# Expert gates built by indirect accumulating transfers into tables in device memory, with all down rounds ahead of all up rounds

## What is computed

```python
q = (xt @ w_query).reshape(T, 8, 2, 128)                      # T = 256 tokens
scores = einsum('thpc,hpnc->thpn', q, sub_keys)               # 128 keys per half
vals, idx = lax.top_k(scores, 16)
cand = vals[..., 0, :, None] + vals[..., 1, None, :]          # 256 sums per head
top_vals, top_c = lax.top_k(cand.reshape(T, 8, 256), 16)
experts = i1 * 128 + i2                                       # 128 of 16384 per token
gates = softmax(top_vals)
y = sum_e gates[e] * gelu(expert_down[e] . x) * expert_up[e]
```

## Time and profile before

| | |
|---|---|
| median of 3 runs | 3400.38 us |
| the profiled execution | 3400.34 us |
| its span | 3398.5 us |
| PE busy | 3264.6 us (96%) |
| DVE, ACT, POOL busy | 59%, 44%, 11% |
| DMA | 594.66 MB, mean 175 GB/s |

### The profile page before, as it was taken

How to read it: one execution, slowest core, us unless ns; L and a number is a source line. 1 busy time by engine, 2 the same in 40 slices (tenths; PEclk the granted TensorE clock), 3 DMA queues, 4 the chain that set the end, 5 groups by cost and what they waited for, 6 DMA issues and landing times.

```text
span 3398.5 us, 43470 instructions
## 1 busy us (share of the span) xinstructions
PE 3264.6 (96%) x16266; PEld 2680.6 (79%) x16266; DVE 2016.6 (59%) x2347; ACT 1478.9 (44%) x1868; POOL 378.7 (11%) x261
## 2 busy tenths in 40 slices
PE   8999999988889999999889999999989999999998
PEld 7988787766667878888767888899877888888886
DVE  5444453898886454555887555655566554444444
ACT  5444344433334343433334434454545544434343
POOL 3100000000881000000783000000000000000000
PEclk9999899999999999999999999999999999999999
DMA  6644355555446666666445766665434555565554
GB/s 210 181 138 127 106 167 167 171 182 182 140 149 205 194 204 190 224 204 192 144 146 191 217 201 199 197 205 160 125 120 138 190 185 181 185 187 182 186 179 148
DMA packets 169433, 594.66 MB, mean 175 GB/s; under 512 B 19739, under 2 KB 20389, under 8 KB 168880
## 3 DMA queue, kind: packets, MB, share of 16 engines
q1 hardware_dynamic: 156544, 549.79, 52.6%
q10 hardware_dynamic: 9456, 33.71, 2.8%
q0 software_dynamic: 3264, 8.82, 0.9%
HBM read 571.00 MB, written 21.23 MB: 174 GB/s over the span
## 4 chain that ended last, share of the span: by engine, by line
PE 81%; DVE 13%; ACT 3%; issue 2%; DMA 0%; POOL 0%; ACTq 0%; DVEq 0%; POOLq 0%
PE ps L1634 18%; PE ps L1635 18%; PE ps L1636 18%; PE ps L1785 7%; PE ps L1786 7%; PE ps L1787 7%; DVE w_lo L538 5%; DVE one L1281 2%; ACT w_hi L533 1%; PE ps L1737 1%; PE ps L1896 1%; PE ps L1907 1%; DVE big L1194 1%; DVE big L1197 1%; DVE big L1196 0%
## 5 line engine op out<-in xcount | busy, mean ns | idle before, releaser
L538 DVE TENSOR_TENSOR w_lo<-raw,w_hi 128x1024 fp32r<-128x1024 f32 (+2 forms) x1072 | 1320.6, 1234 | 1231.1 <-ACT w_hi L533 1228.1
L533 ACT ACTIVATE w_hi<-raw 128x1024 fp32r<-128x1024 f32 (+2 forms) x1072 | 1106.9, 1034 | 1597.2 <-PE ps L1636 1163.5
L1634 PE MATMUL ps<-w_hi,x_hi 128*128 128x512 f32 x1504 | 612.4, 407 | 18.9 <-DVE w_lo L538 18.9
L1634 PE MATMUL ps<-w_hi,a_hi 128*128 128x512 f32 x1536 | 611.0, 398 | 2.6 <-issue 2.6
L1636 PE MATMUL ps<-w_hi,a_lo 128*128 128x512 f32 x1536 | 607.9, 396 | 1.9 <-issue 1.9
L1635 PE MATMUL ps<-w_lo,a_hi 128*128 128x512 f32 x1536 | 608.1, 396 | 0.0
L1635 PE MATMUL ps<-w_lo,x_hi 128*128 128x512 f32 x1504 | 600.3, 399 | 0.0
L1636 PE MATMUL ps<-w_hi,x_lo 128*128 128x512 f32 x1504 | 599.1, 398 | 0.0
L1785 PE MATMUL ps<-w_hi,x_hi 128*128 128x440 f32 (+2 forms) x1184 | 454.0, 383 | 3.3 <-DVE x_lo L1030 3.3
L498 POOL TENSOR_TENSOR one<-is,gate_b 128x512 bf16<-128x512 bf16 x192 | 330.6, 1752 | 1038.7 <-DVE is L1283 1038.7
L1786 PE MATMUL ps<-w_lo,x_hi 128*128 128x440 f32 (+2 forms) x1184 | 440.9, 372 | 0.0
(11 more groups left out here) (338 smaller groups left out, 1921.4 us busy)
## 6 DMA issues: line engine op xcount, KB each, us to landing
raw<-in_peer_down SPq DMA_DIRECT2D x256, 512.0 KB, 3.7
raw<-in_peer_up SPq DMA_DIRECT2D x256, 512.0 KB, 4.1
raw<-in_w_mlp_in SPq DMA_DIRECT2D x128, 512.0 KB, 3.6
raw<-in_w_mlp_out SPq DMA_DIRECT2D x128, 512.0 KB, 3.5
raw<-in_w_in SPq DMA_DIRECT2D x112, 440.0 KB, 3.5
raw<-in_w_in SPq DMA_DIRECT2D x96, 428.0 KB, 3.3
raw<-in_w_out SPq DMA_DIRECT2D x64, 512.0 KB, 3.5
raw<-in_peer_query SPq DMA_DIRECT2D x32, 512.0 KB, 3.6
```

The lines of the kernel that those rows point to most:

```text
L533: act.activation(w_hi[:, c % RING, 0:2 * n], raw[:, c % RING, 0:2 * n], ACT.Copy).then_inc(hi_made, 1)
L538: nc.vector.tensor_tensor(w_lo[:, c % RING, 0:2 * n], raw[:, c % RING, 0:2 * n], w_hi[:, c % RING, 0:2 * n].bitcast(F32), ALU.subtract).th ...
L1634: mm(o, xh, wh, start=(k == 0), stop=False)
```

## The change

- The search runs in eight groups of two heads and one token tile, at 14 steps each, over chunks 8 to 119 of the peer section. The query transposes and key scores stand between the first 14 chunks.
- A group yields 32 table positions (`slot_at`) and 32 gates (`slot_gate`) for each of 128 tokens. POOL adds them into two tables in device memory, one for a token tile, of 2,097,152 fp32 numbers each. One indirect transfer adds one number for each partition. There are 128 transfers to each table, and a transfer waits until the one before it to the same table has landed.
- Both tables are cleared first by 16 transfers of 512 KB each, beside in1 and beside out1 and query.
- All eight down rounds come ahead of all eight up rounds. At chunk 20 of the last down round ACT waits for all transfers. Beside the up rounds it loads 512 KB of gates with each hidden block.
- The one-hot batches on DVE, POOL and PE, and their copies on ACT, are gone.
- The attention scores are issued tile by tile, head 0 and head 1 in turn. The same is done at the two score places of the second layer (L2075, L2112).

```diff
+SEARCHES, SEARCH0, SEARCH_STEPS = 8, 8, 14
+SCORES_AT = (3, 4, 6, 7, 9, 10, 12, 13)
...
+        gat = big[:, 0:2048].rearrange("p (i t n) -> p i t n", i=2, t=NT)
...
+        tables = [nc.dram_tensor(f"gates{t}", (32 * P * JJ * P, 1), F32, kind="Internal").ap() for t in range(NT)]
...
+            def scatter(t, slot):
+
+                if slot:
+                    pool.wait_ge(added_gate[t], 16 * slot)
+                nc.gpsimd.indirect_dma_start(
+                    tables[t], bass.IndirectOffsetOnAxis(ap=slot_at[:, t, slot:slot + 1].bitcast(U32), axis=0),
+                    slot_gate[:, t, slot:slot + 1], None, compute_op=ALU.add).then_inc(added_gate[t], 16)
...
-            for half in range(2):
-                base = 32 * half
...
+            for i in range(16):
+                pool.wait_ge(chunk_used, 132 + 3 * i)
+                clear(1, i)
+            pool.wait_ge(zeroed[1], 16 * 16)
+            for step_ in range(P + 16):
+                if step_ < P:
+                    if step_ % 32 == 0:
+                        pool.wait_ge(chosen_made, 2 * (step_ // 32) + 1)
+                    scatter(0, step_)
+                slot = step_ - 16
+                if slot >= 0:
+                    if slot % 32 == 0:
+                        pool.wait_ge(chosen_made, 2 * (slot // 32) + 2)
+                    scatter(1, slot)
...
+            def load_gates(n, buf):
+                if not static(n) or n >= 2:
+                    act.wait_ge(hid_full, n - 1)
+                for t in range(NT):
+                    rows = tables[t].rearrange("(b p n) o -> b p (n o)", b=32, p=P)
+                    act.dma_start(gat[:, buf, t], rows[n]).then_inc(gates_loaded[buf], 16)
...
                             if c == 5:
                                 reload(f + 1)
+                                load_gates(f + 1, 1)
...
+            def first_gates(pos):
+                if pos == 20:
+                    for t in range(NT):
+                        act.wait_ge(added_gate[t], 16 * P)
+                    reload(0)
+                    load_gates(0, 0)
...
+            phase(False, PEER_ROUNDS - 1, 0, False, True, first_gates)
+            phase(True, PEER_ROUNDS, 0, False, True)
+            with act.Fori(1, PEER_ROUNDS - 1) as r:
+                phase(True, PEER_ROUNDS, r, True, True)
...
-            def fill(n, g, local):
-
-                dve.wait_ge(hid_turned, n + 1)
...
+            def fill(f, g):
+
+                dve.wait_ge(gates_loaded[g % 2], 32 * (2 * f + g // 2 + 1))
+                dve.wait_ge(hid_turned, 4 * f + g + 1)
...
-                for j in range(2):
-                    o, at_ = ps[:, 6 + j], slice(HD * j, HD * j + HD)
-                    for t, at, w in ((0, 0, P), (1, P, S)):
...
+                for t, at, w in ((0, 0, P), (1, P, S)):
+                    for j in range(2):
+                        at_ = slice(HD * j, HD * j + HD)
+                        mm(ps[:, 6 + j, at:at + w], qkT[at_, t * P:t * P + P], qkT[at_, S:S + w], start=True, stop=False)
```

More of the change, by code:

```diff
@@ L258, in build @@
             c_parts = sb("c_parts", [80, 2, S], BF16, part)
+        with ExitStack() as part:
+            sb("beside_zero", [P, 3 * KT * S], F32, part)
+            zero = sb("zero", [P, 1024], F32, part)
         with ExitStack() as part:
@@ L486, in _ @@
                                relrow.unsqueeze(1).to_broadcast([SWA_H, 4, TW + 1])).then_inc(rows_stored, 16)
+                if p == 0:
+                    pool.wait_ge(zero_set, 1)
+                if p % 2:
+                    clear(0, p // 2)
             pool.wait_ge(pv_made, PAIRS)
             pool.dma_start(skT, a["peer_sub_keys"]).then_inc(small_loaded, 16)
-            for half in range(2):
-                base = 32 * half
[L493 to L506, removed]
+            pool.wait_ge(chunk_used, 128)
+            pool.wait_ge(zeroed[0], 16 * 16)
+            nc.gpsimd.memset(zero[:], 0.0).then_inc(zero_set, 1)
+            pool.wait_ge(zero_set, 2)
+            for i in range(16):
[12 more added lines that the diff above has]
+                    scatter(1, slot)
             pool.wait_ge(spilled, 16 * 4 * PEER_ROUNDS)
@@ L722, in _, with copy_pq @@
                     root(3)
-            drain_query(3)
-            for g in range(8):
+            def copy_pq(g):
                 act.wait_ge(pq_turned, g + 1)
@@ L1228, in look_up @@
-            def look_up(s, t, part):
-                hot = cand.rearrange("p (n k) -> p n k", k=TOPK)
-                if part == 0:
-                    step(V.tensor_tensor(hot, rank[:, s, t].unsqueeze(2).to_broadcast([P, P, TOPK]),
-                                         iota[:, 0:TOPK].unsqueeze(1).to_broadcast([P, P, TOPK]), ALU.is_equal))
-                if part == 1:
-                    for g in range(PH):
-                        hg = hot[:, TOPK * g:TOPK * g + TOPK, :]
-                        last = V.tensor_tensor(hg, hg, top_f[:, t, 2 * g + s].unsqueeze(1).to_broadcast([P, TOPK, TOPK]), ALU.mult)
-                    step(last)
-                if part == 2:
-                    step(V.tensor_reduce(chosen[:, s, t], hot, AX, ALU.add))
@@ L1287, in _, with look_up @@
-            b0 = sections["peer"][0]
-            def fill(n, g, local):
-                dve.wait_ge(hid_turned, n + 1)
-                pair = ps[:, 4 + 2 * (g % 2):6 + 2 * (g % 2), :].rearrange("p b (k s) -> p (b k) s", s=S)
-                V.tensor_tensor(pair, pair, gates[:, bass.ds(16 * local + 4 * g, 4), :], ALU.mult).then_inc(hid_full, 1)
+            def look_up(s):
+                step(V.tensor_tensor(hot, rank[:, s].unsqueeze(2).to_broadcast([P, 32, TOPK]),
+                                     iota[:, 0:TOPK].unsqueeze(1).to_broadcast([P, 32, TOPK]), ALU.is_equal))
+                for hh in range(2):
+                    hg = hot[:, TOPK * hh:TOPK * hh + TOPK, :]
+                    last = V.tensor_tensor(hg, hg, top_f[:, hh, s].unsqueeze(1).to_broadcast([P, TOPK, TOPK]), ALU.mult)
+                step(last)
+                step(V.tensor_reduce(part_of[:, s], hot, AX, ALU.add))
@@ L1311, in phase @@
                             if c == 5:
[L1312 removed]
+                                fill(f, 0)
                             if c == 6:
@@ L1854, in _, with turn_pq @@
                         x_turn(j)
-            pe.wait_ge(copied_out, after("query")[1])
-            for g in range(8):
+            b0, c0, d0, _ = sections["peer"]
+            def turn_pq(g):
+                pe.wait_ge(copied_out, c0 - 1 if g < 6 else c0)
                 if g >= 2:
```

367 lines of the change are left out of this document (152 added, 215 removed).

## The result

| | before | after |
|---|---|---|
| median | 3400.32 us (4 runs, 3400.19 to 3406.48) | 3264.99 us (4 runs, 3258.26 to 3268.26) |
| profiled execution, its span | 3400.34, 3398.5 us | 3265.33, 3263.5 us |
| mean granted clock in the span | 0.984 | 0.977 |

The ratio is 0.9595 (95%: 0.9577 to 0.9614), 135 us faster. The forecast was 3211 us, 189 us faster.

The account below looks back on a forecast made before the run. PE bounds the kernel, with its idling and half clock. 3400.34 - 170.9 (gap, peer section) - 16.3 (score order) - 6.8 (half clock) + 5 (gates' loads) = 3211 us; range 3185 to 3350 us.

Parts of the forecast that it names:

- gap ahead of the section goes: Between last query chunk and first peer chunk: PE no longer waits for the last query block, -18.0 us.
- peer phases without their excess, transposes and scores: Peer section: search excess, one-hot batches and their waits go, -163.9 us; transposes and key scores return between chunks, +11.0 us.
- scatters: POOL's indirect adds, awaited by ACT at chunk 244: all land in time, so 0 us.
- gates' loads: Up rounds: 512 KB more beside each reload, 0.15 us for each of 32, +5 us.
- score order and half clock in in1, out1: First layer's 16 pairs: products side by side, -16.3 us; half-clock stretches beside late pairs, -6.8 us.
- The search: DVE over 112 peer chunks: 1.06 us a chunk beside 1.23 for weights, hidden under PE's 2.80; counted as nothing.
- The clearing: 32 stores of 512 KB beside in1, out1 and query: no engine waits for them, counted as nothing.
- The rule of a drain at each change of mode: Attention scores: 64 fewer tiling-mode changes, each up to 0.07 us, would give 4.5 us more; left out of the sum.
- I take something near 4 us: Peer section, each step of the scatter chains: near 4 us, above POOL's 3.1 us writes; ends 2.5 and 6.7 us.
- The limit: Last down round: 144 steps have 622 us before ACT's wait at chunk 244, 4.32 us a step.
- The first rival: Last down round: scatters somewhat late, 4.32 to 5.6 us a step, ACT waits, PE stops; 3266 us, chance 0.24.
- the third rival: Up rounds become DMA-bound: later reload landings exceed 0.5 us slack, 48 us instead of 5, 3254 us; chance 0.11.

Follow-up runs that it names:

- the moved kernel: The kernel after with 8 unused fp32 numbers put ahead of `x_hi`, moving the split activations 32 bytes: 3302.57 us, ratio to before 0.9719.
- the kernel with four gate buffers: The kernel after with scatters waiting once per head and the next up round's gates loaded a phase ahead into four buffers: 3137.19 us, ratio 0.9228.

## Why the prediction was right in direction and where its sum failed

The range held the result, by cancellation: the 54 us between 3211 and 3265 are two large terms of opposite sign and some small ones. They are read from the chunks' starts; the second row is what the other rows leave of the peer section.

| step of the prediction | forecast | measured | difference |
|---|---|---|---|
| gap ahead of the section goes | -18.0 | -17.9 (query -20.4, of it -2.6 the chunk) | 0 |
| peer phases without their excess, transposes and scores | -152.9 | -151.6 | +1 |
| scatters | 0 | +110.8 | +111 |
| gates' loads | +5 | +13.5 | +8 |
| score order and half clock in in1, out1 | -23.1 | -28.2 | -5 |
| in2, out2 beside their chunks | 0 | +6.6 | +7 |
| chunk of 512 columns | 0 | -69 (864 x 0.08) | -69 |
| mlp beside its chunks | 0 | +0.5 | +1 |

**What held.** Phase 0 took 98.22 us, which is the plain 87.04 and 11.2, against +11.0 for the transposes and scores. No down phase waited for DVE: PE is busy for all of phases 0 to 6, although DVE reached 78.25 us of the 87.04 in phase 1. The search cost nothing: phases 1 to 6 all took the plain 87.04 us. The clearing cost 2.4 us at most (in1 and out1, put at full clock and 2.72 us a chunk, took 453.7 us in the kernel with the score order alone and 454.2 to 456.1 in those that clear). The score order gave 15 to 20 us against 16.3. For the half clock beside it, -6.8 us was the middle of the range and -12.0 came; stretches that range over 20 us between kernels with the same code there make this chance. The rule of a drain at each change of mode (the Trainium skill, "TensorEngine Tiling (Array Packing)", section "Tiling Modes"), by which 64 changes fewer would have given 4.5 us more, can't be judged by these: 18.6 us in one kernel speaks for it a little, 16.2 in the other (28.2 less 12.0 for the half clock that fell from 27.3 to 3.4 us) against it. The mean of 17.5 us lies nearer to 16.3 than to the 20.8 of that rule.

**The step that failed** is "I take something near 4 us" for the scatters' step. It had the landing too small and nothing for what comes behind it. The kernel without the gates' loads keeps all 256 transfers, and its trace tells when each landed: beside the weights 4.75 us after the start of its issue, and the next transfer to the same table was issued 0.56 us after that, on average. In a single chain the second part is 0.27 us, so the turns on POOL add 0.3 us; most of the miss is the landing itself. Together that is the step of 5.3 to 5.4 us. Over all 144 steps of the kernel after, the quiet end included, it is 4.99 us. The trace of before had no row for an indirect transfer. The limit moved too: with the faster chunks ACT arrived 604 us after the first issue, not 622, 4.19 us a step. (4.99 - 4.19) x 144 = 115 us is ACT's wait. The first rival (a step of 4.32 to 5.6 us, chance 0.24) was the right one, with the right place and sign; by its own rate it gives (4.99 - 4.32) x 144 = 96 us, and the rest is the chunk. That its figure of 3266 us meets the measured 3264.99 is luck: it stood for a step of 4.7 us and 55 us of stall, and the chunk took off 69 us where the longer stall put on 56 and the small terms the rest. Its mechanism is seen as well: a single chain took 5.20 us a step beside the weights and 3.28 us without them, 1.9 us, where the rival had 1.6. About 0.2 us of that is POOL's issue (1.79 on average in the first 16, 1.55 in the last 16). The rule behind it, an engine serving its queues in turn, one packet at a time (the Trainium skill, "DMA: Bandwidth & Descriptors", section "Queues, rings and completion order"), fits these numbers; no run separates it from other effects of traffic.

**The term that was missing** is the chunk. The sum took 2.80 us for every chunk of the kernel after. A kernel's padding is not part of its algorithm, and the diff's line on `fix` looked like bookkeeping. Without it the result would have been 3302.57 us, as the moved kernel shows, 92 us off the forecast.

**Sizes that were off.** The gates' loads: +5 us were worked out from bytes over a stretch, with the ring hiding the rest. But the reload has PE directly behind it, with 0.5 us of slack, as the third rival noted. A landing later by 0.7 us is felt there, 13.5 us over eight phases (7 to 9 in other kernels with the same loads), about a quarter of that rival's 48. The half clock in in2 and out2 grew from 13.7 to 23.9 us, +5 us; in the kernel with four gate buffers, which has the same second layer, it was 17.1 us, and in the kernel after with `x` moved by 32 bytes 10.2 us. So the new program alone doesn't bring it; the cause stays open.

## What to carry to other kernels

In a chain of transfers that wait for one another, cost the step as the time from issue to landing under the traffic that will be there, plus what follows the landing, multiply by the length of the chain, and set that against the time of the first reader; a few tenths a step decided 80 us here. Then ask which of the waits the data need: here one in sixteen, and dropping the others removed a stall of 108 us. Move a load that nobody waits for away from one that somebody does, even where the mean DMA share leaves room. And before believing that a gain comes from the change, compare the time of an untouched piece of work: if it has moved, look at the addresses.

## What the runs showed of the hardware

- A 512-column fp32r matmul took 226.7 ns with the held operand a multiple of 128 bytes (130304, a multiple of 256 as well) behind the moving one within a partition, and 233.3 ns where 32, 64 or 96 bytes are left. It is 3% of PE's time in such chunks, for 32 bytes of padding.
- An indirect transfer of 128 single numbers holds POOL for 0.97 us as a write and for 1.55 us as an add (the least values), and up to 2.0 and 2.6 us beside other work. Alone, one after the other, the steps are 2.40 and 3.28 us; beside the weights, 4.57 and 5.20 us. In a single chain the next one was issued 0.27 us after the landing.
- PE stood from 1236.0 to 1344.2, and its granted clock was 0.50 (1.2 GHz) for 109 us from 1238.6 on, so that the chunks behind the gap began at that level; the 110.8 us are the gap's 108.2 and some 2 us of this.
